# Spreading the reciprocals of softmax sums with transpositions, and letting rotated keys leave in two steps

## The chip, the cores and the metric

The kernel runs on one core of a Trainium2 chip. The metric is device time in microseconds (us) for one execution, median of several runs; lower is better. Engines are named as in the profile: PE is TensorE (PEld its weight loads), DVE is VectorE, ACT is ScalarE, POOL is GpSimd, SP is SyncE, which issues the DMAs.

## The reference, cut to what matters

Two residual attention layers over 1024 tokens of width 1024, then a pooling mixer and a gated feed-forward layer with a short convolution. All of it is float32.

```
layer 0 (even): y = [global GQA 8 heads | window GQA 8 heads, sink + bias | memory attention 4 heads of 128]
layer 1 (odd):  y = [neighbourhood attention 16 heads, bias | memory attention 4 heads of 128]
x = x + (y * silu(gate)) @ w_out         # h = rmsnorm(x) feeds q, k, v and gate
layer 0's global q and k: rmsnorm per head, then 2-D rope
softmax: p = exp(s - max) / sum; o = p @ v
then: final rmsnorm -> pool mixer -> rmsnorm -> conv_ffn -> residual
```

## The kernel before, in words

Activations are kept transposed: 128 features on the partitions, tokens along the free dimension. A float32 product is done as three matmuls of a high and a low part (`three`, L1533 to L1536). ACT makes the high part of each weight tile (WS from WR), POOL or DVE the low part (L2357, L2023).

One planner (`build`) writes a single list `steps`; each engine's program walks that list in order and issues its part of every step, so each engine's queue has a fixed order, and semaphores tie them together. Attention goes in 12 chunks per layer of one or two heads each: four memory chunks of one 128-wide head (kind m), then in layer 0 four global chunks of two heads (kind a, 1024 keys, `wide`) and four window chunks of two heads (kind b), and in layer 1 eight neighbourhood chunks of two heads (kind c, `grid`). Each chunk has four pairs of query tiles (pp = 0 to 3). For each pair and head a stage of `stream` issues: the scores of this job, then (`begin_job`) the transpositions of the probabilities of the job before (`turn`, L1647) and the products with the values of the job before that (`values`, L1671 to L1680), then matmuls of the dense projections (L1534 to L1536) that the planner interleaves. A wide chunk has two such halves per job (`begin_job`, `go_on`) with one score tile each.

Softmax is normalised at the end. For each score tile VectorE takes 1/sum into one column of RD (`recip`, L2131): RD[query, pp % 2, x, head]. When all values of a pair of tiles are summed, `finish` brings these columns to the layout of the output (features on partitions, queries along the free dimension): PE multiplies a column of RD, read as if it were repeated 128/nh times, by the identity (L1691) into bank B_X of PS. With two heads this is four products of 64 output rows, with one head (memory) two products of 128. VectorE multiplies this with the gate (L2155), and the sum of values with that (L2159, or L2163 and L2165, after ScalarE has copied the other half to YB, L1898). The finish of two-head chunks stands between the last values of a job and the next transpositions in PE's queue. The norms use the same product with the identity to spread their 1/root over the partitions (`bcast`, L1721: four or eight products each, two for the memory norm).

B_X, the bank of the spread, is shared with the flips of values and of rope inputs; `until[bank]` is the semaphore value that PE waits for before it writes a bank again. The dense halves alternate between banks 0 and 1 (`at["bank"]`).

Global keys (two halves, `ka` n0 and n1) go through `rope`: PE flips them to token rows, ScalarE, VectorE and POOL normalise and rotate them, and `rope 4` flips them back into bank 0 or 1 (`h.turned`). From there ScalarE writes four copies of 64x512 (both heads, each into both halves of the partitions, L1864 and L1865) and VectorE the four low parts (`key_low`, L2011). Other keys (kinds k and kg) already leave in two steps, `leave` and `other head`, with other work between them in every queue.

Of the kernel before, what the change touches and what calls it, by code (L numbers as in the profile page):

```python
# [28 lines left out]
B_S, B_PT, B_O, B_X = 2, 4, 6, 7  # L29
# [133 lines left out]
def build(nc, d):  # L163
    ctx = ExitStack()
    with ctx:
        def sb(name, shape, dt=F):
            return ctx.enter_context(nc.sbuf_tensor(name, shape, dt))
# [17 lines left out]
        ID = sb("ID", [128, 128])  # L185
# [2 lines left out]
        COL = sb("COL", [128, NCOL])  # L188
        ST = sb("ST", [128, 8, 4])
        RD = sb("RD", [128, 2, 2, 2])  # L190
        SK = sb("SK", [128, 8])
        PCT = sb("PCT", [128, 4, 16])
        SS = sb("SS", [128, 16])
# [101 lines left out]
        def put(*step):  # L295
            steps.append(step)
# [183 lines left out]
        def rope(h):  # L480
            yield False
            yield True
            while at["rope"]:
                yield True
            at["rope"] = True
            h.vt = s_flip.add()
            h.va, h.vd, h.vp = s_ea.n, s_ed.n, s_rs.add()
            s_ea.add(2)
            s_ed.add(2)
            put("rope 1", h)  # L490
            yield False
            h.vp2 = s_rp.n
            s_rp.add(7)
            f1["after"] = (s_rp, h.vp2 + 1)
            put("rope 2", h)
            at["f1"] = False
            yield False
            yield False
            h.vd3 = s_ed.add()
            put("rope 3", h)  # L500
            yield True
            h.vt2 = s_flip.add()
            h.turned = at["bank"] % 2 if h.to[3] == "k" else B_X
            at["bank"] += h.to[3] == "k"
            h.va4, h.vd4 = s_ea.n, s_ed.n
            a, v = OPS[h.to[3]]
            s_ea.add(a)
            s_ed.add(v)
            h.slot_free = slot_free[h.to[1]]
            put("rope 4", h)  # L510
            at["rope"] = False
            rope_end[:] = [s_flip.n, s_ed.n]
            ready[h.to[0]] = [(s_ed, s_ed.n)]
# [170 lines left out]

        def recip(s):
            s_rec.add(1 if s.c.sink is None else 2)
            s.rec = s.c.rec[s.pp] = s_rec.n
            s.spread = spread_at[s.pp % 2]
            put("recip", s)

        def turn_job(job, i):
# [837 lines left out]
        def tensor_program(e):  # L1529
# [19 lines left out]
            for kind, *of in steps:  # L1549
# [50 lines left out]
                elif kind == "rope 4":  # L1600
# [1 line left out]
                    w.wait_ge(s_ed, h.vd3)  # L1602
                    w.wait_ge(*until[h.turned])
                    flip(RA, h.turned).then_inc(s_flip.sem, 1)
                    until[h.turned] = (s_ed, h.vd4 + OPS[h.to[3]][1])

                elif kind == "score":
                    s, = of
# [73 lines left out]

                elif kind == "finish":
                    f, = of
                    nh = f.c.nh
                    w.wait_ge(s_rec, f.rec)
                    w.wait_ge(*until[B_X])
                    for x in (0, 1):
                        for h in range(nh):
                            n = 128 // nh  # L1690
                            m = e.matmul(PS[n * h:n * h + n, B_X, 128 * x:128 * x + 128],  # L1691
                                         RD[:, f.pp % 2, x, h:h + 1].to_broadcast([128, n]), ID[:, :], start=True, stop=True)
                    m.then_inc(s_spread.sem, 1)
                    until[B_X] = (s_fin, f.fin + 1)
                    until[B_O] = (s_fin, f.y if f.c.mem else f.fin + 3)

                elif kind == "sums":
                    nm, = of
                    both = nm.second is not None
                    for j in range(2 if both else 1):  # L1700
                        w.wait_ge(*nm.acc[j])
                    w.wait_ge(s_init, 2)
                    w.wait_ge(*until[B_X])
                    for j in range(2 if both else 1):
                        for t in range(nm.n // 128):
                            a = 1024 * j + nm.base + 128 * t
                            m = e.matmul(PS[:, B_X, 4 * j + t:4 * j + t + 1], PY[:, a:a + 128], ON[:, :], start=True, stop=True)
                    m.then_inc(s_sums.sem, 1)
                    until[B_X] = (s_var, nm.var2 + 1 if both else nm.var)

                elif kind == "bcast":
                    nm, = of
                    both = nm.second is not None
                    if both:
                        w.wait_ge(s_var, nm.var3)
                    else:
                        w.wait_ge(s_pow, nm.rstd)
                    for b, o in [(nm.bank, 4)] + ([(nm.bank + 2, 12)] if both else []):
                        w.wait_ge(*until[b])
                        for t in range(nm.n // 128):  # L1720
                            m = e.matmul(PS[:, b, 128 * t:128 * t + 128], nm.stat[:, o + t:o + t + 1].to_broadcast([128, 128]),  # L1721
                                         ID[:, :], start=True, stop=True)
                    m.then_inc(s_bcast.sem, 1)
                    until[nm.bank] = (s_nd, nm.nd[7]) if not both else (s_pd, blocks[nm.bank - B_S, 7].scaled)
                    if both:
                        until[nm.bank + 2] = until[nm.bank]

                elif kind == "pool mm":
                    n, g, o, u, bank, px = of
                    (h0, l0), (h1, l1_) = weights(u), weights(u + 1)  # L1730
                    for k in (0, 1):
                        w.wait_ge(s_pp, blocks[n, 2 * g + k].lo)
                    w.wait_ge(*until[bank])
                    cols, sl = slice(128 * o, 128 * o + 128), slice(512 * n, 512 * n + 512)
                    three(PS[:, bank, :], h0[:, cols], l0[:, cols], HT[:, 0, 2 * g, sl], HT[:, 1, 2 * g, sl], True, False)
                    three(PS[:, bank, :], h1[:, cols], l1_[:, cols], HT[:, 0, 2 * g + 1, sl], HT[:, 1, 2 * g + 1, sl], False, True).then_inc(s_pm.sem, 1)
                    until[bank] = (s_px, px)

                elif kind == "ffn mm":
                    p, n, j = of  # L1740
                    wh, wl = weights(p.subs[j])
                    end = j == len(p.tiles) - 1
                    bank = p.bank + n if len(p.halves) > 1 else p.bank
                    if j == 0:
                        w.wait_ge(*until[bank])
                    sl = slice(512 * n, 512 * n + 512)
                    for k in range(p.tiles[j]):
                        c = p.k0[j] + k
                        if p.kind == "in":
                            w.wait_ge(*ffn[n].lo[c])  # L1750
                            rh, rl = HT[:, 0, c, sl], HT[:, 1, c, sl]
                        else:
                            w.wait_ge(s_fd, p.ut[c][n])
                            rh, rl = UT[:, c, 0, sl], UT[:, c, 1, sl]
                        o = slice(128 * k, 128 * k + 128)
                        m = three(PS[:, bank, :], wh[:, o], wl[:, o], rh, rl, j == 0 and k == 0, end and k == p.tiles[j] - 1)
                    if end:
                        m.then_inc(s_fm.sem, 1)
                        until[bank] = (s_fd, p.freed)
                    elif n == p.halves[-1]:  # L1760
                        m.then_inc(s_wused.sem, 1)
# [3 lines left out]
        def scalar_program(e):  # L1765
# [13 lines left out]
            for kind, *of in steps:  # L1779
# [74 lines left out]
                elif kind == "rope 4":  # L1854
# [1 line left out]
                    a, b, slot = 512 * h.n, 512 * h.n + 512, h.to[2]  # L1856
                    w.wait_ge(s_flip, h.vt2)
                    w.wait_ge(*h.slot_free)
                    for x in (0, 1):
                        if h.to[3] == "q":  # L1860
                            act(q_at(slot, x, a, b)[HALF[x], :], PS[HALF[x], h.turned, :], scale=s8).then_inc(s_ea.sem, 1)
                        else:
                            hi = k_at(slot, x, 0, a, b)
                            act(hi[HALF[x], :], PS[HALF[x], h.turned, :], scale=1.0).then_inc(s_ea.sem, 1)  # L1864
                            act(hi[HALF[1 - x], :], PS[HALF[x], h.turned, :], scale=1.0).then_inc(s_ea.sem, 1)  # L1865

                elif kind == "exp":
                    s, = of
# [118 lines left out]
        def vector_program(e):  # L1987
# [27 lines left out]
            for kind, *of in steps:  # L2015
# [67 lines left out]
                elif kind == "rope 4":  # L2083
                    h, = of
                    if h.to[3] == "q":
                        put_q(PS[:, h.turned, :], h.to[2], 512 * h.n, 512 * h.n + 512, h.va4)
                    else:
                        for x in (0, 1):
                            key_low(h, PS[:, h.turned, :], x, h.va4 + 2 * x + 2)

                elif kind == "score":
                    s, = of
# [28 lines left out]
                elif kind == "recip":  # L2121
# [7 lines left out]
                        w.wait_ge(s_rec, s.rec - 1)  # L2129
                    w.wait_ge(s_spread, s.spread)  # L2130
                    e.reciprocal(rd, den).then_inc(s_rec.sem, 1)  # L2131

                elif kind == "turn":
                    job, i = of
# [476 lines left out]
```

## Time and profile before

| | |
|---|---|
| median of 3 runs | 2480.85 us (2480.84 to 2481.98) |
| the profiled execution | 2480.93 us, of which the span of its instructions is 2479.1 us |
| mean granted TensorE clock | 0.992 of full |
| PE busy | 2384.5 us, 96% of the span |
| DVE, ACT, POOL busy | 52%, 49%, 37% |
| finishes | 64 of two-head chunks, 32 of memory chunks |

Times are from the start of the span. A matmul's row gives its start and its duration; matmuls are pipelined, so what one costs its neighbours is read from start to start and not from its duration. A row with "x8" merges eight consecutive records of one kind. Layer 0's memory chunks run from about 105 us to 255 us, its global chunks to about 600 us, its window chunks to about 780 us; layer 1's memory chunks start after 900 us and its neighbourhood chunks end at about 1605 us. Behind that come the final norm, the pooling mixer and the feed-forward layer.

### The profile page before, as it was taken

Reading aid. Unit: us, or ns where it says so; the run is one execution under the profiler, and the core shown is the slowest. Engines: PE = TensorE matmul, PEld = TensorE weight load, DVE = VectorE, ACT = ScalarE, POOL = GpSimd, SP = SyncE. Lnnn points to the kernel's source line nnn. Section 1 sums busy time; section 2 is a strip of 40 time slices with the busy share of each in tenths; the row PEclk is TensorE's granted clock in tenths of the full one; section 3 lists DMA queues with packets and bytes.
Section 4 is the critical chain, followed back from the end, with each engine's and each line's share of the span. In section 5 each row is a group of like instructions: output and inputs, shape, how many; then the busy total and the mean of one; then the engine's idle time right before and its main releaser. Section 6 shows DMA issues by size and latency. Waiting matters only on the chain.

```text
span 2479.1 us, 36148 instructions
## 1 busy us (share of the span) xinstructions
PE 2384.5 (96%) x12568; PEld 2017.7 (81%) x12568; DVE 1285.7 (52%) x2665; ACT 1207.7 (49%) x2873; POOL 921.1 (37%) x1133
## 2 busy tenths in 40 slices
PE   7999999999999999999999998999889999999999
PEld 6788787878878878888888887877778888888887
DVE  7344667667775333355555555587966213321331
ACT  6444566566775434455555565554554213322331
POOL 5554322311145642311222223577665323322321
PEclk9999999999999999999999999999999999999999
DMA  7322101111243332322223224432223211111112
GB/s 220 108 69 64 39 22 35 31 33 51 59 135 96 98 115 69 94 71 79 85 80 90 84 81 136 134 88 85 73 86 98 60 47 52 45 50 51 47 48 89
DMA packets 305987, 191.91 MB, mean 77 GB/s; under 512 B 63760, under 2 KB 284176, under 8 KB 305296
## 3 DMA queue, kind: packets, MB, share of 16 engines
q1 hardware_dynamic: 305808, 189.61, 26.0%
q8 instruction: 102, 1.67, 0.3%
q14 instruction: 77, 0.63, 0.1%
HBM read 170.16 MB, written 19.40 MB: 76 GB/s over the span
## 4 chain that ended last, share of the span: by engine, by line
PE 84%; DVE 5%; ACT 3%; issue 3%; POOL 3%; DMA 1%; SPq 1%; POOLq 0%; DVEq 0%; ACTq 0%
PE PS L1534 21%; PE PS L1536 21%; PE PS L1535 21%; PE PS L1680 5%; PE PS L1647 5%; PE PS L1634 3%; PE PS L1635 2%; PE PS L1691 2%; POOL WS L2357 1%; ACT PY L1769 1%; POOL HT L2416 1%; DVE EO L2209 1%; DVE ST L2099 1%; PE PS L1589 1%; PE PS L1671 1%
## 5 line engine op out<-in xcount | busy, mean ns | idle before, releaser
L2357 POOL TENSOR_TENSOR WS<-WR,WS 128x256 fp32r<-128x256 f32 x773 | 595.9, 790 | 1234.3 <-ACT WS L1769 1233.6
L1534 PE MATMUL PS<-HT,WS 128*128 128x512 f32 x1760 | 709.7, 403 | 31.9 <-POOL HT L2416 10.1
L1536 PE MATMUL PS<-HT,WS 128*128 128x512 f32 x1760 | 690.7, 392 | 0.0
L1535 PE MATMUL PS<-HT,WS 128*128 128x512 f32 x1760 | 689.2, 392 | 0.0
L1769 ACT ACTIVATE WS<-WR 128x256 fp32r<-128x256 f32 x788 | 296.1, 409 | 270.0 <-PE PS L1536 234.0
L1534 PEld LDWEIGHTS PS<-HT,WS 128*128 128x128 f32 x1760 | 333.5, 189 | 101.4 <-issue 14.6
L1536 PEld LDWEIGHTS PS<-HT,WS 128*128 128x128 f32 x1760 | 332.5, 189 | 72.5
L1535 PEld LDWEIGHTS PS<-HT,WS 128*128 128x128 f32 x1760 | 333.7, 190 | 63.0
L1769 ACT ACTIVATE PT<-PS 128x512 fp32r<-128x512 f32 x352 | 186.2, 529 | 229.9 <-PE PS L1647 229.7
L1992 DVE TENSOR_TENSOR PT<-PS,PT 128x512 fp32r<-128x512 f32 x352 | 211.2, 609 | 72.8 <-ACT PT L1769 70.0
L1680 PE MATMUL PS<-PT,QKV 128*128 128x256 f32 (+1 forms) x1248 | 207.3, 287 | 3.2 <-DVE YB L2163 2.2
L2357 POOL TENSOR_TENSOR PT<-WR,PT 128x256 fp32r<-128x256 f32 (+1 forms) x166 | 134.9, 828 | 202.3 <-ACT PT L1769 202.2
L1769 ACT ACTIVATE QKV<-PS 64x512 fp32r<-64x512 f32 (+2 forms) x208 | 121.7, 585 | 149.0 <-PE PS L1536 130.7
L1680 PEld LDWEIGHTS PS<-PT,QKV 128*128 128x128 f32 x1248 | 179.0, 191 | 10.6 <-ACT PT L1769 3.6
L1647 PE MATMUL PS<-ID,PY 128*128 128x128 f32 x1072 | 185.8, 277 | 0.0
L1534 PE MATMUL PS<-QKV,WS 128*128 128x512 f32 (+1 forms) x380 | 143.1, 377 | 7.5 <-DVE WS L2023 3.6
L1993 DVE SCALAR_TENSOR_TENSOR QKV<-PS,QKV 64x512 fp32r<-64x512 f32 (+1 forms) x112 | 77.2, 689 | 130.9 <-ACT QKV L1769 128.8
L1535 PE MATMUL PS<-QKV,WS 128*128 128x512 f32 (+1 forms) x380 | 141.7, 373 | 0.0
L1536 PE MATMUL PS<-QKV,WS 128*128 128x512 f32 (+1 forms) x380 | 141.6, 373 | 0.0
L1634 PE MATMUL PS<-QKV 128*128 128x384 f32 (+2 forms) x320 | 121.6, 381 | 14.4 <-ACT PY L1769 10.6
L1534 PE MATMUL PS<-HT,PT 128*128 128x512 f32 x320 | 126.5, 395 | 7.1 <-POOL WS L2357 4.2
L1647 PEld LDWEIGHTS PS<-ID,PY 128*128 128x128 f32 x1072 | 124.4, 140 | 10.9 <-issue 10.5
(192 smaller groups left out, 3717.5 us busy)
## 6 DMA issues: line engine op xcount, KB each, us to landing
WR<-in_ffn_in SPq DMA_DIRECT2D x120, 256.0 KB, 2.9
WR<-in_w_in_odd SPq DMA_DIRECT2D x106, 256.0 KB, 3.0
EO<-in_grid SPq DMA_DIRECT2D x48, 384.0 KB, 3.1
WR<-in_w_in_even SPq DMA_DIRECT2D x100, 128.0 KB, 2.5
WR<-in_w_out_odd SPq DMA_DIRECT2D x48, 256.0 KB, 2.9
yd<-PY SPq DMA_DIRECT2D x44, 256.0 KB, 2.9
WR<-in_w_in_even SPq DMA_DIRECT2D x34, 256.0 KB, 2.9
WR<-in_w_out_even SPq DMA_DIRECT2D x64, 128.0 KB, 2.8
```

What stands on the lines that cost most here:

```text
L1534: e.matmul(out, wh, rh, start=start, stop=False)
L1535: e.matmul(out, wh, rl, start=False, stop=False)
L1536: return e.matmul(out, wl, rh, start=False, stop=stop)
L1634: e.matmul(out, q, kh, start=True, stop=False)
L1635: m = e.matmul(out, q, kl, start=False, stop=True)
L1647: m = e.transpose(PS[:, B_PT + pb, o + 128 * z:o + 128 * z + 128], p_at(job.c, job.scores[x].slot, p0, p0 + 128), ID[:, :])
L1680: m = e.matmul(out, vv, p, start=a, stop=b)
L1691: m = e.matmul(PS[n * h:n * h + n, B_X, 128 * x:128 * x + 128], RD[:, f.pp % 2, x, h:h + 1].to_broadcast([128, n]), ID[:, :], start=True, ...
L1769: return e.activation(out, in_, func, **more)
L1992: return e.tensor_tensor(out, src, f32(hi), ALU.subtract)
L1993: return e.scalar_tensor_tensor(out=out, in0=src, scalar=scale, in1=f32(hi), op0=ALU.mult, op1=ALU.subtract)
L2357: e.tensor_tensor(ws(i, 1, n), RAW[raw_slot(u)][:, o:o + n], f32(ws(i, 0, n)), ALU.subtract).then_inc(s_wlop.sem, 1)
```

## The change

Three edits. (1) `finish` spreads with two transpositions (`e.transpose`, as in `turn`) for every kind of chunk. For memory chunks the transposed operand is the RD column, read as if repeated 128 times. For two-head chunks it is a block of a new tile RW [128, 256]: once per pair of tiles, behind the last of its four reciprocals, VectorE copies the four columns of RD into RW, each repeated 64 times, and adds one to `s_rec`, which `finish` waits for. The copy waits for the finish before it (`s.before`). (2) `bcast` of the norms spreads with transpositions too. (3) `rope 4` of keys issues the copies of the first head; a new step `other keys` issues those of the second head one planner step later; the bank stays taken until both are out.

```diff
+        RW = sb("RW", [128, 256])
...
-            a, v = OPS[h.to[3]]
-            s_ea.add(a)
-            s_ed.add(v)
+            s_ea.add(2)
+            s_ed.add(2)
             h.slot_free = slot_free[h.to[1]]
             put("rope 4", h)
+            h.vd5 = s_ed.n
+            if h.to[3] == "k":
+                yield False
+                h.va5 = s_ea.n
+                s_ea.add(2)
+                h.vd5 = s_ed.add(2)
+                put("other keys", h)
...
         def recip(s):
             s_rec.add(1 if s.c.sink is None else 2)
-            s.rec = s.c.rec[s.pp] = s_rec.n
-            s.spread = spread_at[s.pp % 2]
+            s.rec = s_rec.n
+            s.spread, s.before = spread_at[s.pp % 2], s_spread.n
+            s.wide = s.x == 1 and s.h == 1
+            s_rec.add(1 if s.wide else 0)
+            s.c.rec[s.pp] = s_rec.n
             put("recip", s)
...
-                    until[h.turned] = (s_ed, h.vd4 + OPS[h.to[3]][1])
+                    until[h.turned] = (s_ed, h.vd5)
...
                     for x in (0, 1):
-                        for h in range(nh):
-                            n = 128 // nh
-                            m = e.matmul(PS[n * h:n * h + n, B_X, 128 * x:128 * x + 128],
-                                         RD[:, f.pp % 2, x, h:h + 1].to_broadcast([128, n]), ID[:, :], start=True, stop=True)
+                        r = RD[:, f.pp % 2, x, 0:1].to_broadcast([128, 128]) if f.c.mem else RW[:, 128 * x:128 * x + 128]
+                        m = e.transpose(PS[:, B_X, 128 * x:128 * x + 128], r, ID[:, :])
...
-                            m = e.matmul(PS[:, b, 128 * t:128 * t + 128], nm.stat[:, o + t:o + t + 1].to_broadcast([128, 128]),
-                                         ID[:, :], start=True, stop=True)
+                            m = e.transpose(PS[:, b, 128 * t:128 * t + 128], nm.stat[:, o + t:o + t + 1].to_broadcast([128, 128]), ID[:, :])
...
-                    for x in (0, 1):
-                        if h.to[3] == "q":
+                    if h.to[3] == "q":
+                        for x in (0, 1):
                             act(q_at(slot, x, a, b)[HALF[x], :], PS[HALF[x], h.turned, :], scale=s8).then_inc(s_ea.sem, 1)
-                        else:
-                            hi = k_at(slot, x, 0, a, b)
-                            act(hi[HALF[x], :], PS[HALF[x], h.turned, :], scale=1.0).then_inc(s_ea.sem, 1)
-                            act(hi[HALF[1 - x], :], PS[HALF[x], h.turned, :], scale=1.0).then_inc(s_ea.sem, 1)
+                    else:
+                        for y in (0, 1):
+                            act(k_at(slot, 0, 0, a, b)[HALF[y], :], PS[HALF[0], h.turned, :], scale=1.0).then_inc(s_ea.sem, 1)
+
+                elif kind == "other keys":
+                    h, = of
+                    for y in (1, 0):
+                        act(k_at(h.to[2], 1, 0, 512 * h.n, 512 * h.n + 512)[HALF[y], :], PS[HALF[1], h.turned, :], scale=1.0).then_inc(s_ea.sem, 1)
...
                     else:
-                        for x in (0, 1):
-                            key_low(h, PS[:, h.turned, :], x, h.va4 + 2 * x + 2)
+                        key_low(h, PS[:, h.turned, :], 0, h.va4 + 2)
+
+                elif kind == "other keys":
+                    h, = of
+                    key_low(h, PS[:, h.turned, :], 1, h.va5 + 2)
...
                     e.reciprocal(rd, den).then_inc(s_rec.sem, 1)
+                    if s.wide:
+                        w.wait_ge(s_rec, s.rec)
+                        w.wait_ge(s_spread, s.before)
+                        r = RD[:, s.pp % 2, :, :].rearrange("p x (h o) -> p (x h) o", o=1)
+                        e.tensor_copy(RW.rearrange("p (a n) -> p a n", n=64), r.to_broadcast([128, 4, 64])).then_inc(s_rec.sem, 1)
```

## Rows read from the trace of the kernel before

**Rows 1.** The page, parts 1 and 4: busy time; the chain by engine.

```profile
PE 2384.5 (96%) x12568; PEld 2017.7 (81%) x12568; DVE 1285.7 (52%) x2665; ACT 1207.7 (49%) x2873; POOL 921.1 (37%) x1133
...
PE 84%; DVE 5%; ACT 3%; issue 3%; POOL 3%; DMA 1%; SPq 1%; POOLq 0%; DVEq 0%; ACTq 0%
```

**Rows 2.** Busy time by stretch: length, then PE, PEld, DVE, ACT, POOL (instructions), clock, DMA.

```profile
230.00:600.00 370.00, 352.87 (x2156) 300.43 (x2155) 241.69 (x430) 222.37 (x451) 93.14 (x117) 0.99 0.13 34
...
1130.00:1600.00 470.00, 461.59 (x2641) 397.35 (x2640) 271.32 (x790) 276.76 (x705) 128.86 (x162) 1.00 0.32 97
```

**Rows 3.** Groups of PE's instructions by form: busy us, mean ns | idle before.

```profile
L1691 PE MATMUL PS<-ID,RD 128*64 128x128 f32 x512 | 42.0, 285 | 2.6 <-DVE QKV L1992 1.6 <-DVE QKV L1993 0.5
```

**Rows 4.** Timeline of PE in a neighbourhood chunk: start, duration, engine, line.

```profile
1300.18 0.66 PE L1691 MATMUL PS<-ID,RD 128*64 128x128 f32 x8
1300.76 0.44 PE L1647 MATMUL PS<-ID,PY 128*128 128x128 f32 x2
1300.96 0.48 PE L1534 MATMUL PS<-HT,WS 128*128 128x512 f32 x1
...
1308.18 0.60 PE L1647 MATMUL PS<-ID,PY 128*128 128x128 f32 x4
1308.53 0.64 PE L1680 MATMUL PS<-PT,QKV 128*128 128x128 f32 x4
```

**Rows 5.** Timeline of PE in a global chunk.

```profile
516.98 0.66 PE L1691 MATMUL PS<-ID,RD 128*64 128x128 f32 x8
...
517.98 0.47 PE L1534 MATMUL PS<-HT,WS 128*128 128x512 f32 x1
...
519.44 0.39 PE L1634 MATMUL PS<-QKV 128*128 128x512 f32 x1
```

**Rows 6.** Timeline of ACT in the same stage.

```profile
517.23 0.78 ACT L1769 ACTIVATE YB<-PS 64x256 f32<-64x256 f32 x2
...
519.05 0.19 ACT L1769 ACTIVATION_READ_ACCUMULATOR PY<-PS,ST 128x1 f32 x1
```

**Rows 7.** Timeline of PE in a memory chunk.

```profile
165.65 0.60 PE L1647 MATMUL PS<-ID,PY 128*128 128x128 f32 x4
166.09 0.61 PE L1691 MATMUL PS<-ID,RD 128*128 128x128 f32 x4
166.46 0.48 PE L1534 MATMUL PS<-HT,WS 128*128 128x512 f32 x1
...
171.75 0.76 PE L1534 MATMUL PS<-HT,WS 128*128 128x512 f32 x1 [3.65 <-DVE SG L2040]
```

**Rows 8.** Timeline of PE at a norm of 512 tokens, and at the final norm.

```profile
38.45 1.05 PE L1721 MATMUL PS<-ID,SS 128*128 128x128 f32 x8
39.25 0.36 PE L1534 MATMUL PS<-WS,QKV 128*128 128x256 f32 x1
...
1637.87 2.05 PE L1721 MATMUL PS<-ID,SS 128*128 128x128 f32 x16
1639.68 0.48 PE L1534 MATMUL PS<-HT,WS 128*128 128x512 f32 x1
```

**Rows 9.** Groups of DVE's instructions by form.

```profile
L2131 DVE RECIPROCAL RD<-ST 128x1 f32<-128x1 f32 x320 | 37.9, 152 | 2.2
...
L2165 DVE TENSOR_TENSOR PY<-YB,SG 128x256 f32<-128x256 f32 x40 | 18.9, 472 | 1.4
```

**Rows 10.** Timeline of DVE behind the second half of the rotated keys.

```profile
165.67 2.85 DVE L1992 TENSOR_TENSOR QKV<-PS,QKV 64x512 fp32r<-64x512 f32 x4 [2.68 <-ACT QKV L1769]
168.54 0.76 DVE L2099 TENSOR_REDUCE ST<-PS 128x1 f32<-128x256 f32 x2
...
170.92 0.68 DVE L2040 SCALAR_TENSOR_TENSOR SG<-SG,PS 128x512 f32<-128x512 f32 x1
```

**Rows 11.** Busy time by stretch, columns as in Rows 2.

```profile
171.50:174.50 3.00, 2.75 (x7) 2.21 (x8) 0.10 (x1) 0.00 (x0) 1.11 (x2) 0.50 0.67 192
...
512.00:588.00 76.00, 72.95 (x463) 61.30 (x463) 51.61 (x87) 46.25 (x91) 8.88 (x12) 1.00 0.13 34
```

More of the change, by code:

```diff
@@ L1684, in tensor_program @@
                     f, = of
-                    nh = f.c.nh
                     w.wait_ge(s_rec, f.rec)
```

## The prediction

> **What bounds the kernel now.** I read the page first. PE is busy for 96% of the span and makes up 84% of the chain that ended last [rows 1], so in most places time taken from PE's queue is time taken from the kernel. Busy time by stretch then says where this is not quite so [rows 2]: while the neighbourhood chunks run, PE is idle for 8.4 of 470 us, and while the global chunks run, for 17 of 370 us. Last I read the timelines around each kind of finish, from start to start, because durations of matmuls overlap.
>
> A point that decides the case: a product with the identity leaves two records, a transposition one. The 64 two-head finishes hold 4 products each in the code, 256, and 512 records in the trace [rows 3], eight per finish in the timeline; the four transpositions of a bank of four blocks are four records [rows 4]. They cost PE accordingly. Eight records, 64 columns wide, take 1300.18 to 1300.76, 0.58 us, or 0.145 a product. Four transpositions take 1308.18 to 1308.53, 0.35 us [rows 4].
>
> **Two-head finishes, sum for PE.** In the neighbourhood chunk the products and the two transpositions behind them last from 1300.18 to the dense matmul at 1300.96, 0.78 us. After the change four transpositions stand there, 0.35 us. Saved: 0.43 us. This is more than the products' 0.58 less two transpositions, because what follows products also starts a little late (two transpositions take 0.20 behind them). In the global chunk products and four transpositions last from 516.98 to 517.98, 1.00 us [rows 5]; with the first four transpositions at 0.35 and two more at 0.11 each (the pair above took 0.20 for two) that becomes 0.57, again 0.43 saved.
>
> Window and neighbourhood chunks have 12 x 4 = 48 finishes: 48 x 0.43 = 20.6 us. PE waits for almost nothing near them, and ACT and DVE are busy for under 60% of that stretch [rows 2], so I count all of it.
>
> The 16 finishes of the global chunks are different. The score tile behind the dense matmuls needs the banks that ScalarE's exponential empties. It starts at 519.44 [rows 5]; the exponential's read-out ends at 519.05 + 0.19 = 519.24 [rows 6]. Where PE truly waits for this, it starts 0.05 us behind the read-out's end. So only 0.15 us of the 0.43 can be had there: the exponential stands behind ScalarE's two YB copies, which start at 517.23 and wait for the values, not for the spread [rows 6]. Going through the timeline I find 12 of the 16 in this state, one where PE waits already, and three with room: 12 x 0.15 + 0 + 3 x 0.43 = 3.1 us. If the whole 0.43 came it would be 6.9, if nothing 0; both ends stay in the range.
>
> **Memory finishes.** From the first of the four transpositions to the dense matmul 165.65 to 166.46, 0.81 us, with two products of 128 columns (four records, 166.09 to 166.46, 0.18 us a product) in it [rows 7]. After: six transpositions, 0.57. Saved 0.24, times 32: 7.7 us.
>
> **Norms.** Four products take 38.45 to 39.25, 0.80 us; four transpositions 0.35: 0.45 saved, six times (two for the first norm, two for layer 1's, two for the feed-forward's): 2.7. The final norm's eight products take 1637.87 to 1639.68, 1.81 us [rows 8], against 0.35 + 4 x 0.11 = 0.79: 1.02, twice. Together 4.7 us. VectorE waits for several of these, so it gains the same time.
>
> **The fill of RW.** 64 copies of 128x256 on DVE. The trace has no such copy. Its bounds: the shortest instruction of that queue, the reciprocal at 0.15 us, and a two-input operation on SBUF of the same size, 0.47 us [rows 9]; I take 0.35, since it writes 256 columns but reads four. That is 22 us more on DVE (10 to 30). It is queued behind the reciprocals of a job; behind it stand the next job's maxima and low parts, for which ACT and then PE wait. The finish that needs it comes one whole job later in PE's queue, five to eight us, so PE doesn't wait for the fill, and the finish that it waits for is one job old. The cover is missing where the stream is drained (the ends of the global, window and neighbourhood chunks): three times fill plus hand-over, 3 x 0.5 = 1.5 us lost. In the global stretch DVE is busy for 65% [rows 2] and a maximum is now and then just in time; I leave 1 us for that.
>
> **Keys in two steps.** Only two instances. At the first no PE wait stands near. At the second, PE waits for 3.65 us until 171.75 [rows 7]: the next dense half needs the bank of the gate half just done, its gate needs DVE L2040 at 170.92, and before this DVE made four key parts from 165.67 for 2.85 us, then the maxima at 168.54, for which the exponentials and, behind them on ACT, the gate's tanh waited [rows 10]. With two parts, DVE is free 2.85 / 2 = 1.43 us sooner and everything to 171.75 moves by that; the other two parts come behind the gate's. The bank they hold is next needed a whole dense half later, over five us. Gain 1.4 us (bounds: 0, if other work takes the place, and 2.85, if all four parts got out of the way).
>
> **Sum.** 20.6 + 3.1 + 7.7 + 4.7 + 1.4 = 37.5 us, less 2.5 for fill and drains. PE's other waits end by POOL, DVE or a DMA whatever PE does; they are about 90 us in all, and some of what PE gains just ahead of one is lost in it. I take 2 us. 37.5 - 4.5 = 33 us. The sum is made against the profiled execution, 2480.93 us, which is the median's 2480.85 for all purposes: about 2448 us.
>
> **The clock.** PE's clock fell to 0.50 between 171.5 and 174.5, behind the wait of 3.65 us; between 512 and 588, where the planner puts transpositions into every stage as in [rows 5], it stayed at 1.00 [rows 11]. At 0.50 seven matmuls took 3.0 us where they take 0.24 each otherwise (six from 517.98 to 519.44 [rows 5]): about 1.3 us lost per such stretch. The shorter wait may spare this one, or another wait may grow one; that is +-3 us. The Trainium skill, "TensorE: Matmul & The Clock Gate", Part 4: PE-mode transpose, says that transposing doesn't count as work for the gate in the same way as a product. By that rule each finish would weaken the clock's case; the trace gives no sign of it, with clock 1.00 in a stretch that transposes in every stage.
>
> **The rivals.**
> Transposing a repeated column or a filled block may be no quicker than a product. Then the two 128-wide transpositions cost what a memory finish's two products cost, about 0.37 us against 0.58: 48 x 0.21 + 2 (global chunks) = 12 us, nothing for memory and norms; with keys and losses the time is 2481 - 12 - 1.4 + 4.5 = 2472. For it: no transposition in the trace reads with stride zero. Against: the products do, at 0.145 us for two records. 6%.
>
> All waits behave as in the global chunks. Every finish gives only 0.15: 96 x 0.15 = 14.4, norms half, 2.4, keys 1.4, less 3: 2466 us. For it: fixed order, and one queue late holds the rest. Against: 98% PE busy among the neighbourhood chunks [rows 2]. 12%.
>
> A transposition of a repeated column may be cheaper than one of probabilities: a quarter of the 0.18 us product [rows 7], 0.05 instead of 0.11, so 96 x 2 x 0.06 = 12 us more, 2436. Against: every transposition seen, spaced 0.10 to 0.11 behind its like. 3%. The Trainium skill's page named above, Terms, calls the transpose mode four times as fast for float32, which is this rival; the trace doesn't agree so far (0.18 against 0.11).
>
> The slow side: the clock. If PE falls to half speed behind finishes because they hold no product any more, each costs 1.3 us. The gain of 33 us is gone after 25 of the 96; behind every second one, 48 x 1.3 = 62 us, 2510 us. For it: a finish now stands directly beside other transpositions, six in a row in memory chunks. Against: [rows 11]. 3%.
>
> **How the numbers follow.** The forecast, 2448 with its own range 2441 to 2456, has 76%. The rivals have 12, 6, 3 and 3%. The range that should hold the time 8 times in 10 is 2438 to 2461. It takes in 6.9 or 0 for the global finishes, the fill between its bounds, the clock's +-3 and half the way to the waits' rival. A measurement of this kernel can tell about 0.2%, 5 us: faster by more 94%, within it 3%, slower 3%.
>
> **What would show it.** L1691's records give way to two transpositions per finish, 192 in all, and L1721's 84 records to 42. In neighbourhood chunks the distance from the last values to the dense matmul falls from 0.78 to 0.35. In global chunks PE begins to wait, some 0.25 us, for ScalarE's exponential behind a finish. A new DVE group of 64 copies of 128x256 at 0.2 to 0.45 us, with no PE wait named for it but at drains. The wait of 3.65 us is about 2.2. I am wrong if the finish's two transpositions are spaced by 0.18 or more, if PE waits for the fill in steady state, or if new stretches of clock 0.50 begin without an idle PE before them.

## The result and the profile after

| | median | runs | against before |
|---|---|---|---|
| before | 2481.41 us | 2480.84 to 2483.43 | |
| changed | 2451.14 us | 2444.50 to 2452.59 | ratio 0.9873, 95% interval 0.9861 to 0.9885 |

The change saves 30 us where 33 were forecast (2448, range 2438 to 2461). The profiled execution took 2452.28 us, with a span of 2450.4.

The page of the changed kernel, parts 1 and 4, answers to [rows 1]: PE has 490 records fewer and is as busy as before in share, so it is still the bound. 490 is 640 + 84 records of products less 192 + 42 transpositions.

```profile
PE 2352.4 (96%) x12078; PEld 1996.2 (81%) x12078; DVE 1305.0 (53%) x2729; ACT 1205.5 (49%) x2873; POOL 919.7 (38%) x1133
...
PE 82%; DVE 5%; ACT 4%; issue 4%; POOL 4%; DMA 1%; SPq 0%; POOLq 0%; DVEq 0%; ACTq 0%
```

The groups by form, PE's finishes and VectorE's fill (busy us, mean ns, idle before):

```profile
L1699 PE MATMUL PS<-ID,RW 128*128 128x128 f32 x128 | 25.7, 282 | 2.3 <-DVE QKV L2002 1.1 <-DVE QKV L2003 0.5 <-DVE RW L2149 0.4
L1699 PE MATMUL PS<-ID,RD 128*128 128x128 f32 x64 | 12.3, 273 | 1.1 <-DVE QKV L2003 0.7 <-DVE QKV L2002 0.4
```
```profile
L2149 DVE COPY RW<-RD 128x256 f32<-128x256 f32 x64 | 20.0, 313 | 2.2
```

Now a finish in a neighbourhood chunk, PE's timeline after. It answers to [rows 4]:

```profile
1278.14 0.64 PE L1690 MATMUL PS<-PT,QKV 128*128 128x128 f32 x4
1278.62 0.41 PE L1699 MATMUL PS<-ID,RW 128*128 128x128 f32 x2
1278.87 0.38 PE L1657 MATMUL PS<-ID,PY 128*128 128x128 f32 x2
1279.01 0.47 PE L1544 MATMUL PS<-HT,WS 128*128 128x512 f32 x1
```

And before, the row of the values ahead of the products of [rows 4], which I had not read closely enough:

```profile
1299.61 0.64 PE L1680 MATMUL PS<-PT,QKV 128*128 128x128 f32 x4
```

From the finish to the dense matmul: 0.78 us before (1300.18 to 1300.96), 0.39 after. But the values ahead of it also take less, 0.48 instead of 0.57 us (1278.14 to 1278.62; 1299.61 to 1300.18). From the values to the dense matmul it is 1.35 before and 0.87 after: 0.48 us a finish.

A global chunk, PE then ACT, after; this answers to [rows 5] and [rows 6]:

```profile
513.48 0.38 PE L1699 MATMUL PS<-ID,RW 128*128 128x128 f32 x2
...
515.89 0.50 PE L1644 MATMUL PS<-QKV 128*128 128x512 f32 x1 [0.20 <-ACT PY L1775]
516.22 0.39 PE L1645 MATMUL PS<-QKV 128*128 128x512 f32 x1
```
```profile
513.82 0.78 ACT L1775 ACTIVATE YB<-PS 64x256 f32<-64x256 f32 x2
...
515.64 0.20 ACT L1775 ACTIVATION_READ_ACCUMULATOR PY<-PS,ST 128x1 f32 x1
```

PE is done earlier and then waits 0.20 us: the exponential's read-out ends at 515.84, PE starts at 515.89. Counted from the values to the score tile, all 16 finishes do what the forecast says: 12 gain 0.14 to 0.16 us, one nothing, three 0.42, 0.53 and 0.55, together 3.3. But the wait costs more than its length. The first score matmul behind it takes 0.33 us to the next (515.89 to 516.22), where before, without a wait, it took 0.23 (519.44 in [rows 5] to 519.67):

```profile
519.67 0.40 PE L1635 MATMUL PS<-QKV 128*128 128x512 f32 x1
```

Counted to the end of the score tile, the 12 keep 0.01 to 0.05 us each, and the 16 together 1.9 (the sum from e5's trace, where the same 12, one and three stand). Who waited for whom, PE's queue in the global chunks (255 to 600), before and after: twelve waits more, 2.6 us more.

```profile
PE PS L1634 <- ACT PY L1769: 10.6, 14, 2.0
```
```profile
PE PS L1644 <- ACT PY L1775: 13.2, 26, 2.0
```

The wait behind the second half of the rotated keys [rows 7, 10] did not shrink as forecast in this execution. ACT's timeline, then PE's:

```profile
164.44 0.42 ACT L1775 ACTIVATE WS<-WR 128x256 fp32r<-128x256 f32 x1 [3.63 <-DMA WR<-in_w_in_even]
164.76 1.19 ACT L1775 ACTIVATE QKV<-PS 64x512 fp32r<-64x512 f32 x2
```
```profile
170.55 0.77 PE L1544 MATMUL PS<-HT,WS 128*128 128x512 f32 x1 [3.46 <-DVE SG L2050]
```

The keys do leave two at a time, but a weight split ahead of them in ACT's queue waited for a DMA, so they left (164.76) more than 1 us after PE had flipped them (163.02 to 163.37).

### The profile page after: what moved, and what is told of

Its sections match the earlier page's. It is cut to its first block, busy times and chain, and to the rows that moved or that the text cites. A ratio compares the mean times of both kernels' runs of the same rounds, so it can differ in the third digit from the quotient of the medians.

```text
span 2450.4 us, 35232 instructions
## 1 busy us (share of the span) xinstructions
PE 2352.4 (96%) x12078; PEld 1996.2 (81%) x12078; DVE 1305.0 (53%) x2729; ACT 1205.5 (49%) x2873; POOL 919.7 (38%) x1133
## 4 chain that ended last, share of the span: by engine, by line
PE 82%; DVE 5%; ACT 4%; issue 4%; POOL 4%; DMA 1%; SPq 0%; POOLq 0%; DVEq 0%; ACTq 0%
PE PS L1544 21%; PE PS L1546 21%; PE PS L1545 21%; PE PS L1690 5%; PE PS L1657 5%; PE PS L1644 3%; PE PS L1645 2%; POOL WS L2375 2%; ACT PY L1775 1%; PE PS L1699 1%; POOL HT L2434 1%; POOL PT L2375 1%; PE PS L1599 1%; DVE EO L2227 1%; PE PS L1681 1%
## 5 line engine op out<-in xcount | busy, mean ns | idle before, releaser
L1544 PE MATMUL PS<-HT,WS 128*128 128x512 f32 x1760 | 709.4, 403 | 32.4 <-POOL HT L2434 10.1
L1644 PE MATMUL PS<-QKV 128*128 128x384 f32 (+2 forms) x320 | 123.6, 387 | 17.2 <-ACT PY L1775 13.2
L1775 ACT ACTIVATE PY<-PY,ST 128x384 f32<-128x384 f32 (+1 forms) x192 | 115.6, 602 | 37.4 <-DVE ST L2132 25.5
```

The source lines that it names most:

```text
L1544: e.matmul(out, wh, rh, start=start, stop=False)
L1644: e.matmul(out, q, kh, start=True, stop=False)
L1775: return e.activation(out, in_, func, **more)
```

## The experiments

Times are medians. e1 to e4, e5 to e8, and e9 with e10 each ran together on one chip beside the same runs of the kernel before. "Saved" is against before; its interval comes from the ratio's, times 2482.

| run | us | before | saved (95% interval) |
|---|---|---|---|
| e1 two-head finishes only | 2459.67 | 2482.52 | 22.8 (18.6 to 25.6) |
| e2 memory finishes and norms only | 2468.13 | 2482.52 | 14.4 (9.4 to 16.6) |
| e3 keys in two steps only | 2479.27 | 2482.52 | 3.2 (1.2 to 5.7) |
| e4 changed, keys at once | 2449.85 | 2482.52 | 32.7 (27.8 to 35.7) |
| e5 changed kernel again | 2450.16 | 2482.51 | 32.4 (27.8 to 34.3) |
| e6 changed, exponential first | 2450.96 | 2482.51 | 31.6 (28.0 to 34.3) |
| e7 changed, each transposition twice | 2461.94 | 2482.51 | 20.6 (14.9 to 21.6) |
| e8 fill of RW only | 2482.84 | 2482.51 | -0.3 (-4.0 to 0.2) |
| e9 two products from RW | 2471.99 | 2483.18 | 11.2 (6.9 to 13.2) |
| e10 changed, global chunks with products | 2451.31 | 2483.18 | 31.9 (28.0 to 35.5) |

A second view is sharper than the medians. I take the time between the same two dense matmuls of PE's queue in the profiled executions, as it is independent of where the clock fell elsewhere. It is one execution of each kernel, and it is sharp only where no stretch at half clock lies inside. The clean one is 1129 to 1525 us (before), 24 finishes of neighbourhood chunks, full clock in every run. Computed from the start times, saved against before there: e1, e4, e5, e6, e10 and the changed kernel 11.4 us each; e2, e3 and e8 0.0; e9 5.4; e7 6.6.

**e1, the two-head finishes alone.** Edit: the change's fill and two transpositions for two-head chunks; memory and norms keep this, and the keys leave at once:

```diff
+                        if f.c.mem:
+                            m = e.matmul(PS[:, B_X, 128 * x:128 * x + 128], RD[:, f.pp % 2, x, 0:1].to_broadcast([128, 128]), ID[:, :], start=True, stop=True)
+                        else:
+                            m = e.transpose(PS[:, B_X, 128 * x:128 * x + 128], RW[:, 128 * x:128 * x + 128], ID[:, :])
```

> The kernel before with only the two-head finishes changed: VectorE fills RW, PE transposes it twice; memory finishes and norms keep their products, the rotated keys leave at once. Theory (PE's queue pays per record): 48 finishes at 0.40 to 0.43 us and 16 global ones at 0.15 to 0.2 give 20 to 23 us: about 2459. Rival (the waits swallow it, as in the global chunks): 64 x 0.15 = 10 us, 2471. Rival (the fill on VectorE hurts): above 2465, with PE waits named for RW outside the drains.

22.8 us: the theory holds. 11.4 of them come in the clean stretch alone, 0.475 a finish, which agrees with the 0.48 read above. In the window chunks (603 to 785 us, 15 finishes, full clock in both traces) it is 5.6 us, 0.37 a finish.

**e2, memory finishes and norms alone** (transpositions in `finish` of memory chunks and in `bcast`, no RW).

> The kernel before with only the memory finishes and the norms spread by transpositions; two-head finishes keep four products and there is no RW. Theory: 32 x 0.23 + 6 x 0.45 + 2 x 0.97 = 12 us, about 2469. Rival (waits swallow): half of it, 2475. If the two parts of runs 1 and 2 add up to less than the whole change gained, something else in the change (the keys) gained; if to more, they take from each other.

14.4 us by the medians, 13.9 in the spans of the profiled executions (2479.1 - 2465.2). The 12 expected are inside the interval, half of it is not. Not all of it is the edit's: 2.7 us of the 13.9 fall between 254 and 785 us, in global and window chunks, which e2 leaves as they were; before has two stretches at half clock there, e2 one. In the two stretches of memory chunks, with equally long half clock in both traces, it saves 3.0 and 3.2 us, 0.20 a finish.

**e3 and e4, the keys.** e3 is before with `rope 4` and `other keys` of the change; e4 is the changed kernel without the `yield False` between them:

```diff
             if h.to[3] == "k":
-                yield False
                 h.va5 = s_ea.n
```

> The kernel before with only the keys in two steps. Theory of the prediction: the wait of 3.65 us near 168 shrinks to about 2.2, the span by 1.4 us, 2479.5. Rival (seen in the trace after, where the wait was still 3.46 us because ScalarE's split ahead of the keys waited for a weight DMA that landed late): no gain, 2481, and the wait by the DMA stands ahead of the key copies here too.

> The changed kernel with the keys leaving at once again (all else changed). If the keys' two steps carry 1.4 us, it is at 2452.5; if the DMA takes that back, it is within 1 us of 2451, and the wait near 167 us is about as long as before.

e3 is faster by its interval, and its trace shows the mechanism as forecast: PE's wait is 2.14 us (2.2 forecast).

```profile
169.91 0.47 PE L1544 MATMUL PS<-HT,WS 128*128 128x512 f32 x1 [2.14 <-DVE SG L2055]
```

In e4's trace that wait is 3.88 us. So my rival for e3 fell: the late DMA is not tied to the edit. But it was not a matter of one execution either. With the keys in two steps PE waited 2.14 to 2.58 us in e3, e5, e6 and e7, but 3.26 us in e10, where ScalarE's weight split ahead of the keys again waited for a DMA (3.20 us, until 163.55). What the keys bring thus depends on when that weight lands. Next to the other edits their gain can't be told from nothing by the medians (e4 2449.85, e5 2450.16): 1.5 us is less than these resolve. The traces do tell: between the same dense matmuls around it (106 to 254 us, one stretch of equal length at half clock in each) e3 saves 1.3 us, and e5 saves 1.5 more than e4 (4.5 against 3.0). Where the weight was late, it is 0.7 (e10) and 0.5 (the first profiled execution) more than e4. The 3.2 us of e3's median are more than that; its interval takes 1.3 in.

**e5, the changed kernel again.**

> The changed kernel itself, timed beside runs of the kernel before on one chip with the next three. If the parts simply add (22.8 for two-head finishes, 14.4 for memory finishes and norms, 3.2 for the keys, each alone), it should be 40 us under before, 2442. If part of it is given back, as the first timing says (30 us) and as the kernel with the keys at once says (33 us), it is again near 2450; theory: what is given back is mostly PE time at 0.50 of its clock, so its slower runs show a granted clock of 0.990 and less, its faster ones 0.992.

32.4 us, between the first timing and the sum of the parts. The granted clock of each run shows why these few us are hard to pin down. Of the 41 runs of the kernel before, the 18 at clock 0.990 have a median of 2483.3 us and the 12 at 0.992 one of 2479.5. Of the changed kernel's eight runs, five were at 0.990 (median 2450.0), one at 0.992 (2444.5), two below (2452.6, 2454.3). At equal clock the change is worth 33 us (at 0.990) or 35 (at 0.992, by one run). Two stretches at half clock in the first profiled execution that before did not have:

```profile
320.80:323.80 3.00, 3.00 (x13) 2.67 (x11) 2.60 (x6) 0.03 (x1) 0.00 (x0) 0.50 0.03 8
327.60:330.60 3.00, 3.00 (x14) 2.82 (x13) 1.23 (x1) 0.54 (x2) 0.00 (x0) 0.50 0.00 0
```

Both follow waits of PE for ScalarE, 1.56 us to 320.41 and 1.78 us to 326.77. Waits of the same length stand in the same places in other executions with the clock left at 1.00, e5's among them.

**e6, the exponential ahead of the YB copies.**

```diff
-                    if value_all(old, left[1], left[1] + 1):
+                    last = value_all(old, left[1], left[1] + 1)
+                    early = last and old.c.wide and len(news) == 1
+                    if early:
+                        exps(news[0])
+                        news = ()
+                    if last:
                         finish(old.c, old.pp)
```

> The changed kernel, in global chunks ScalarE's exponential for the next score tile now stands ahead of its two YB copies of the finish instead of behind them; nothing else moves on any other engine. Theory (in global chunks the YB copies of 0.78 us hold the exponential, and this holds PE's next score tile, so that 12 finishes keep only 0.15 of 0.4 us): PE's waits of 0.2 us about 2.3 us behind a finish vanish, 12 x 0.25 = 3 us faster than the changed kernel, 2447 to 2448. Rival (ScalarE as a whole is the bound in these stages): the wait moves to the next score tile and the time stays at 2451. Second rival (the YB copies free the bank of the sums later, so PE's next values wait): slower, 2454.

No faster. PE's waits behind finishes for the exponential go from 25 back to 12 (260 to 600 us), but a new one comes, seven times, for the bank of the sums. VectorE's addition (L2186) frees that bank, and it waits for the YB copies, which now come later. Who waited for whom there:

```profile
PE PS L1649 <- ACT PY L1780: 8.5, 12, 2.0
...
PE PS L1695 <- DVE YB L2186: 2.7, 7, 0.6
```

So the order of these two in ScalarE's queue did hold the score tile: up to it, 11 of the 12 finishes now gain 0.50 to 0.53 us instead of 0.15. And the second rival has the mechanism right: the wait moves to the values. Its 2454 is not reached; 2450.96 can't be told from e5's 2450.16.

**e7, every transposition of a finish twice.**

```diff
+                        for _ in (0, 1):
                             m = e.transpose(PS[:, B_X, 128 * x:128 * x + 128], r, ID[:, :])
```

> The changed kernel with every transposition of a finish made twice into the same place: 192 more transpositions and no product more. Theory (PE pays 0.11 us per transposition in its queue): 80 finishes x 2 x 0.11 = 17.6 us more, and in global chunks the 16 x 0.22 partly inside PE's waits, 1 to 3: 19 to 21 us slower than the changed kernel, 2470. Rival (the clock counts transpositions as no work): new stretches at half clock near finishes, some 1.5 us each, over 2480, granted clock under 0.988.

11.8 us slower than e5 by the medians, less than the 19 to 21 expected. In the clean stretch 24 x 2 transpositions cost 11.4 - 6.6 = 4.8 us, 0.10 each, as the theory says. The rest of the miss is outside it. In global chunks PE's added waits are gone again (254 to 603 us: idle 17.4 us, before 17.1, changed 19.9), as the second pair fits into them. And most of the miss is the clock: four of its six runs were at 0.991 to 0.994, three of e5's four at 0.990. Set against runs of the changed kernel at the same clock, e7 is 17.3 us slower at 0.990 (two runs) and 16.5 at 0.992 (two against one).

The clock's rival has fallen: with 384 transpositions in the finishes the granted clock was not lower but higher than in the changed kernel, and the profiled execution has 8 stretches at half clock before the end, the changed kernel's two have 12 and 10. The Trainium skill, "TensorE: Matmul & The Clock Gate", Part 4: PE-mode transpose, says that a transposition doesn't count as a busy TensorE in the same way. By that the clock should have been lower in e7; these runs show no such cost in a queue where dense matmuls stand around the transpositions.

**e8, the fill alone** (RW filled and waited for, products as before).

> The kernel before with only the fill of RW on VectorE added (64 copies of 0.29 us and the wait of each finish for it); finishes, norms and keys as before. Theory (VectorE's queue has room nearly everywhere): 0 to 1.5 us slower than before. Rival (in the global chunks VectorE is 65% busy and its maxima are just in time, so each of those fills costs): 16 x 0.3 = 5 us slower. The time that it costs is also the part of the two-head gain of 22.8 us that another place for the fill could give back.

0.3 us slower by the medians, 0.0 in the clean stretch: there VectorE's queue hides the fill. PE waited for RW once in the whole trace, 0.4 us. The interval (4.0 us slower to 0.2 faster) leaves out the rival's 5 us, but not a cost of some us.

**e9, two full-width products from RW.**

```diff
+                            m = e.matmul(PS[:, B_X, 128 * x:128 * x + 128], RW[:, 128 * x:128 * x + 128], ID[:, :], start=True, stop=True)
```

> The kernel before with RW filled by VectorE, and the two-head finishes made by two products of 128 columns with RW instead of two transpositions or four products of 64; memory finishes, norms and keys as before. It parts the two things that the change does at once: fewer instructions, and transpositions in place of products. Theory (a product leaves two records and costs PE 0.18 us at 128 columns, a transposition 0.11, and what follows products starts 0.03 to 0.06 late): per finish 0.587 falls to 0.37 us, 48 x 0.21 + 2 = 12 us, about 2470; in the neighbourhood chunks about half of what transpositions gave. Rival (only the number of instructions counts): as fast as the two-head change alone, 2460. Rival (a full-width product costs as much as two half ones): no gain, 2482.

11.2 us where 12 were expected, 5.4 of 11.4 in the clean stretch. PE's timeline of e9:

```profile
1311.54 0.64 PE L1689 MATMUL PS<-PT,QKV 128*128 128x128 f32 x4
1312.01 0.66 PE L1700 MATMUL PS<-ID,RW 128*128 128x128 f32 x4
1312.51 0.38 PE L1656 MATMUL PS<-ID,PY 128*128 128x128 f32 x2
1312.65 0.48 PE L1543 MATMUL PS<-HT,WS 128*128 128x512 f32 x1
```

Two products still take 0.50 us (1312.01 to 1312.51), two transpositions 0.25. So half of the two-head gain is fewer and wider instructions, for which RW is needed, and half is transposing. The start times show more of this. Behind the first of them, the records of e9's two products follow each other by 0.11 us, as the records of transpositions do: here a record of a full-width product costs PE what a transposition costs, and there are twice as many. And the neighbours are no slower than beside transpositions: the values ahead take 0.47 us (0.57 before, 0.48 changed) and the two transpositions behind 0.14 (0.20 before, 0.14 changed). Nor is it the repeated column: ahead of a memory finish, whose products of 128 rows read one, four transpositions take 0.44 us before ([rows 7], 165.65 to 166.09) and 0.44 after. So what slowed the neighbours before was the products of 64 output rows, not products as such.

**e10, products kept in the global chunks.**

> The changed kernel, but the 16 finishes of the global chunks keep their four products and there is no fill there. Theory (12 of these 16 kept only 0.15 us because ScalarE's exponential holds the next score tile): 2 to 3.5 us slower than the changed kernel, 2453, and PE's waits of 0.2 us behind these finishes are gone. Rival (the global chunks gain as the others do): 6.5 us slower, 2457. Rival (the fill on VectorE costs more there than the transpositions bring): no slower, 2450.

The waits are those of before again (10.6 us, 14 times), as expected. The time is 0.5 us less saved than e5's, on another chip: nothing that can be told from none. By the stretch of the global chunks (254 to 603 us) e5 saves 4.0 us and e10 also 4.0, but before has two short stretches at half clock there, e5 one and e10 none, so much of both is the clock. With one in each, e2, e3 and e8, which keep the products, save 1.6 to 1.8 us there, and e4 and e5, which transpose, 3.7 and 4.0: about 2 us more, which agrees with the 1.9 read from the score tiles.

## Why the prediction was right, point by point

- **PE is the bound, and a product leaves two records:** right. e1 and e2 each give what their records say.
- **48 finishes of window and neighbourhood chunks, 20.6 us:** the mechanism is right, the size too low. I read the distance from the first product on and missed 0.09 us that the values ahead of these products take longer. Measured is 0.475 a finish in the clean stretch, but 0.37 among the window chunks in e1's trace: some 21 to 23 us for 48.
- **Global chunks, 3.1 us:** the state was read right: 12 waits of 0.20 us appeared where 12 were counted, and up to the score tile the 16 gain 3.3 us. What is kept is about 1.9, since the first matmul behind each new wait takes 0.10 us longer, which the sum did not hold.
- **Memory finishes 7.7 and norms 4.7 us:** 12.4 together, e2 measured 14.4 (9.4 to 16.6), of which 2 to 3 us are the clock's and other waits'. From one dense matmul to the next around it a memory finish gains 0.23 us as forecast; over the stretches 0.20 of it is kept, 6.4 us for 32 instead of 7.7.
- **The fill:** 0.31 us each, between its bounds of 0.15 and 0.47 and near the 0.35 chosen. PE waited for it once, 0.4 us. The 2.5 us that I took off for fill and drains were probably too many; e8 shows -0.3 with an interval from -4.0 to 0.2, and its trace one wait.
- **Keys, 1.4 us:** right by e3's trace (the wait falls from 3.65 to 2.14 us, the stretch by 1.3) and by e5 against e4 (1.5); a third to a half of it in the two executions where a weight was late.
- **Losses by other waits, 2 us, and the clock's +-3:** the clock was the larger. Over the whole span PE idles 98.0 us instead of 94.6, and 2.8 of these 3.4 us are in the global chunks.
- **The rivals:** no quicker transposition of repeated columns: fell (two take 0.25 us, two products 0.50). Everything waits as in the global chunks: fell, 0.475 and 0.37 a two-head finish elsewhere. Four times as cheap: fell, 0.10 to 0.11 each. Clock lost to transpositions: fell (e7); all new stretches at half clock in the first profiled execution stand behind a wait of PE.

That 33 came so near is in part luck. The memory and the global term were 1.3 and 1.2 us too high, and 2.5 us were taken off for a fill that shows no such cost; these errors go opposite ways.

What stays open: the parts alone give 22.8 + 14.4 + 3.2 = 40.4 us, the whole 30 to 33. The clock is one reason. Four of e2's five runs were at 0.992, and against the runs before at that clock they save 11.5 us; four of e3's at 0.992 save 1.4, five at 0.991 save 2.6; three of e1's at 0.990 save 24.2. That makes 37 to 38, against 33 to 35 for the whole at equal clock. Whether the remaining 2 to 5 us are lost because the parts take from each other is not shown. The spans of e1 and e2 do add up to e4's (20.7 + 13.9 against 34.3), but e1's trace has 51.6 us at half clock and the others 38 to 41, so that sum proves nothing. No run here controlled where the clock fell.

## What to carry to other kernels

Where PE is the bound, spread a float32 column over the partitions by transposing a repeated column or a filled block: 0.10 to 0.13 us for 128x128, where a product with the identity takes 0.18 to 0.25. Avoid products of 64 output rows for this: here four of them also slowed what stood ahead of and behind them, by 0.09 and 0.05 us. Read an operation's price from the start of what precedes it to the start of what follows it. Before counting a saving, look for the next wait behind it: where that wait is released by another engine whose queue does not depend on the saved work, only the slack counts, and less than that if the first instruction behind the new wait is slower, as here. Turning that engine's order around can just move the wait.

## What the runs showed of the hardware that was not expected

Matmuls ahead of float32 products of 64 output rows also cost more: the four values took 0.57 us ahead of these, 0.48 ahead of transpositions and 0.47 ahead of products of 128 (e9). The first score matmul behind a wait of 0.20 us took 0.33 us to the next, without a wait 0.23. VectorE's copy of four columns to 256, each repeated 64 times, took 0.29 us in the median and 0.31 in the mean. In the traces here PE's clock fell to 0.50 behind waits of PE (but for the last us of the span), the shortest of them 1.06 us; but in e8, once (at 786.8), only waits of 0.38, 0.22 and 0.39 us stood ahead (784 to 786 us). Waits of equal length did not always bring it down. Runs of the kernel before at 0.990 of granted clock took 3.8 us longer than those at 0.992, more than any of the smaller edits here brought.
